# A two-model f32 kernel: norm statistics as four columns, latents read raw by ScalarE, convolution work dealt anew

## What is computed

```python
for l in range(2):
    p = rmsnorm(x, g_mix[l]) @ w_in[l]            # 384 | 256 | 32 | 2 x 512 columns
    c_q, c_kv = rmsnorm(p[:, :384], g_q[l]), rmsnorm(p[:, 384:640], g_kv[l])
    q = c_q @ w_uq[l]; k_nope, v = split(c_kv @ w_ukv[l])
    k_rope = rope(p[:, 640:672]);  a, gt = split(p[:, 672:])
    y_attn = softmax((q . [k_nope, k_rope]) / sqrt(96)) @ v       # 8 heads
    u = dwconv31(a * sigmoid(gt)) + b;  u = silu(layernorm(u))
    x = x + concat(y_attn, u) @ w_o[l]
    z = dwconv3(rmsnorm(x, g_ffn[l]) @ w_up[l]); x = x + (silu(zg) * zv) @ w_down[l]
x = rmsnorm(x, g_final)
```

## Time and profile before

| | us |
|---|---|
| median of 3 runs | 3025.79 |
| lowest and highest | 3019.03, 3028.0 |
| the profiled execution | 3028.47 |
| its span | 3026.7 |
| TensorE matmul busy in the span | 2827.2 (93%) |
| VectorE busy | 1775.7 (59%) |
| GpSimd busy | 1764.7 (58%) |
| ScalarE busy | 777.0 (26%) |

### The profile page before, as it was taken

How to read it: one execution, slowest core, us unless ns; L and a number is a source line. 1 busy time by engine, 2 the same in 40 slices (tenths; PEclk the granted TensorE clock), 3 DMA queues, 4 the chain that set the end, 5 groups by cost and what they waited for, 6 DMA issues and landing times.

```text
span 3026.7 us, 35770 instructions
## 1 busy us (share of the span) xinstructions
PE 2827.2 (93%) x12832; PEld 2291.1 (76%) x12832; DVE 1775.7 (59%) x1941; ACT 777.0 (26%) x1256; POOL 1764.7 (58%) x1000
## 2 busy tenths in 40 slices
PE   6898899999787999989999989999999998899998
PEld 5676788887676888877776778888777777788876
DVE  8884566428855666256656557054666665842644
ACT  2332222102423222023555312011222221310202
POOL 5983566667944766654443447666553343566663
PEclk9998999999998999999999989999999998899999
DMA  3111222232011322322111113222221111232221
GB/s 134 56 43 49 77 97 97 99 104 91 28 36 55 110 95 95 106 79 73 63 63 56 63 65 108 93 95 97 77 90 62 56 56 50 76 99 96 97 98 49
DMA packets 66367, 237.36 MB, mean 78 GB/s; under 512 B 7152, under 2 KB 7408, under 8 KB 66224
## 3 DMA queue, kind: packets, MB, share of 16 engines
q1 hardware_dynamic: 65392, 234.00, 23.2%
q10 hardware_dynamic: 832, 1.51, 0.2%
HBM read 233.38 MB, written 2.10 MB: 78 GB/s over the span
## 4 chain that ended last, share of the span: by engine, by line
PE 77%; DVE 12%; DVEq 5%; issue 3%; ACT 2%; DMA 0%; ACTq 0%; SPq 0%
PE ps L457 23%; PE ps L463 22%; PE ps L460 22%; PE ps L1013 2%; PE ps L579 1%; DVE ps L1594 1%; DVE qw L2224 1%; PE ps L802 1%; DVEq L2226 1%; PE ps L1049 1%; PE ps L805 1%; DVE rstd L1567 1%; DVE ssum L1498 1%; DVE ssum L2072 0%; DVE x_lo L1486 0%
## 5 line engine op out<-in xcount | busy, mean ns | idle before, releaser
L398 POOL TENSOR_SCALAR w_hi<-w_raw 128x1024 fp32r<-128x1024 f32 x437 | 481.2, 1101 | 1193.3 <-PE ps L457 1182.5
L400 POOL TENSOR_TENSOR w_lo<-w_raw,w_hi 128x1024 fp32r<-128x1024 f32 x437 | 1108.8, 2537 | 36.4
L457 PE MATMUL ps<-x_hi,w_hi 128*128 128x512 f32 x2024 | 817.9, 404 | 74.1 <-DVE x_lo L2110 16.3
L463 PE MATMUL ps<-x_hi,w_lo 128*128 128x512 f32 x2024 | 797.8, 394 | 0.0
L460 PE MATMUL ps<-x_lo,w_hi 128*128 128x512 f32 x2024 | 797.8, 394 | 0.0
L457 PEld LDWEIGHTS ps<-x_hi,w_hi 128*128 128x128 f32 x2024 | 386.0, 191 | 177.0 <-issue 33.8
L460 PEld LDWEIGHTS ps<-x_lo,w_hi 128*128 128x128 f32 x2024 | 386.7, 191 | 83.5 <-issue 5.5
L463 PEld LDWEIGHTS ps<-x_hi,w_lo 128*128 128x128 f32 x2024 | 385.9, 191 | 82.9
L457 PE MATMUL ps<-a_hi,w_hi 128*128 128x512 f32 x512 | 201.8, 394 | 0.0
L463 PE MATMUL ps<-a_hi,w_lo 128*128 128x512 f32 x512 | 201.0, 393 | 0.0
L460 PE MATMUL ps<-a_lo,w_hi 128*128 128x512 f32 x512 | 199.2, 389 | 0.0
(11 more groups left out here) (377 smaller groups left out, 4566.6 us busy)
## 6 DMA issues: line engine op xcount, KB each, us to landing
w_raw<-wts SPq DMA_DIRECT2D x437, 512.0 KB, 3.3
xres<-xT SPq DMA_DIRECT2D x2, 1024.0 KB, 8.8
outT<-xres SPq DMA_DIRECT2D x1, 2048.0 KB, 7.1
pf<-pT ACTq DMA_DIRECT2D x2, 512.0 KB, 3.5
prm<-prm SPq DMA_DIRECT2D x1, 452.0 KB, 3.9
lev<-levels ACTq DMA_DIRECT2D x1, 384.0 KB, 3.1
wtmp<-pos SPq DMA_DIRECT2D x1, 128.0 KB, 3.1
ident<-identity SPq DMA_DIRECT2D x1, 64.0 KB, 10.6
```

Of the source, the lines that this page charges most:

```text
L398: nc.gpsimd.tensor_scalar(w_hi[:, s, :], w_raw[:, s, :], 1.0, 0.0, ALU.mult, ALU.add).then_inc(w_rounded[s], 1)
L400: nc.gpsimd.tensor_tensor(w_lo[:, s, :], w_raw[:, s, :], w_hi[:, s, :].bitcast(F32), ALU.subtract).then_inc(w_split[s], 1)
L457: mm = nc.tensor.matmul(out, whi, xhi, start=first, stop=False)
L463: return nc.tensor.matmul(out, wlo, xhi, start=False, stop=last)
```

## The change

Statistics of the first model. The sums are made as four columns: TensorE multiplies the 128x128 pieces of the sum tile by one column of ones (row_stat); root and reciprocal are taken on 128x4 tiles (rowm); TensorE spreads the four factor columns over a bank with the identity (row_factor), and the users read the factor from that bank. For statistic 0 ScalarE copies it to rstd. The spread of statistic 0 stands in the middle of input tile 1, that of 1 behind tile 7, that of 2 behind tile 10, that of 3 behind output block n = 2, that of 4 right behind its sum. The mixer's sum tile is kept in root, since statistics 1 and 2 add a multiple of it.

Latents. The kv and q tiles are taken raw from PSUM by ScalarE, multiplied with their gain (taken), and squared from PSUM too. The mixer's factor drops out of their norm but for the eps, which the added multiple of the sum tile stands for (ecol, ebias). VectorE multiplies them by their factor only.

Convolution. GpSimd has channel tile 2 in place of 1, and its taps are behind blocks 15, 17, 18 and 19. VectorE has 0, 1 and 3; 45 of its 96 steps a layer stand ahead of the first query, where 39 did. The third key tile goes to bank 5 in place of 0.

```diff
@@ -83,10 +83,10 @@
 VW = VDIM + 1
-K_BANK = [2, 3, 0, 1]
-POOL_CH = 1
-CONV_BY_DVE = [0, 2, 3]
-POOL_TAPS = {10: 1, 11: 1, 12: 1, 13: 1, 15: 2, 17: 10, 18: 8, 19: 7}
+K_BANK = [2, 3, 5, 1]
+POOL_CH = 2
+CONV_BY_DVE = [0, 1, 3]
+POOL_TAPS = {15: 3, 17: 12, 18: 9, 19: 7}
@@ -474,8 +476,27 @@
+            def row_stat(out, l, k, extra=None):
+                pe.wait_ge(sum_ready, l * 6 + (k + 1))
+                for tt in range(TT):
+                    c = slice(tt * P, (tt + 1) * P)
+                    mm = nc.tensor.matmul(out[:, tt:tt + 1], (root if k <= 0 else ssum)[:, c], ones[:, 0:1], start=True,
+                                          stop=extra is None)
+                    if extra is not None:
+                        mm = nc.tensor.matmul(out[:, tt:tt + 1], root[:, c], ecol[:, extra, :], start=False, stop=True)
+                mm.then_inc(stat_ready, 1)
+            def row_factor(out, n):
+                pe.wait_ge(root_used, n + 2)
+                for tt in range(TT):
+                    mm = nc.tensor.matmul(out[:, tt * P:(tt + 1) * P], rowm[:, 1, tt:tt + 1].to_broadcast([P, P]), ident[:, :],
+                                          start=True, stop=True)
+                mm.then_inc(factor_ready, 1)
             BU = [0, 0, 0, 0]
-            for n in ([t % 4 for t in range(W_IN)] + K_BANK + [0] * (HEADS + HEADS // 2)
+            for n in ([t % 4 for t in range(W_IN)] + [b for b in K_BANK if b < 4] + [0] * (HEADS + HEADS // 2)
                       + [b for b in W_O_BANK if b < 4] + [m % 4 for m in range(KD + 2 * FT)]):
@@ -490,23 +511,30 @@
                             pe.wait_ge(x_split, l * 2 * KD + (kt + 1))
+                        if t == 1 and kt == 5:
+                            row_factor(ps[4], l * 5)
                         mm = three(ps[b][:, :], w_hi[:, s, kt * P:(kt + 1) * P], w_lo[:, s, kt * P:(kt + 1) * P],
...
                     if t == 0:
-                        stat(ps[4][:, :], l, 0)
+                        row_stat(ps[4], l, 0)
                     if t == 6:
-                        pe.wait_ge(root_ready, l * 5 + 1)
-                        stat(ps[4][:, :], l, 1)
+                        pe.wait_ge(rstd_ready, l + 1)
+                        row_stat(ps[4], l, 1, 0)
+                    if t == 7:
+                        row_factor(ps[4], l * 5 + 1)
+                    if t == T_KR:
+                        pe.wait_ge(kvn_ready, l * KKV + KKV)
+                        row_stat(ps[4], l, 2, 1)
                     if t == T_KR + 1:
-                        pe.wait_ge(root_ready, l * 5 + 2)
-                        stat(ps[4][:, :], l, 2)
+                        row_factor(ps[4], l * 5 + 2)
...
                 for i, b in enumerate(K_BANK):
-                    bank(b, l * BU[b] + 1)
+                    if b < 4:
+                        bank(b, l * BU[b] + 1)
                     for kt, s in ((0, s0), (1, s1)):
@@ -649,10 +677,12 @@
                     if n == 1:
-                        stat(ps[7][:, :], l, 4)
-                pe.wait_ge(root_ready, l * 5 + 4)
-                stat(ps[4][:, :], l, 5)
+                        row_stat(ps[7], l, 4)
+                    if n == 2:
+                        row_factor(ps[7], l * 5 + 3)
+                row_stat(ps[4], l, 5)
+                row_factor(ps[4], l * 5 + 4)
                 first_up = []
@@ -1096,32 +1125,44 @@
-                def sqrt(bank, k, n, widen=1):
+                def sqrt(bank, k, n, bias, widen=1):
...
                     act.wait_ge(root_used, lr + (k + 1))
-                    nc.scalar.activation(root[:, :], bank, ACT.Sqrt, bias=(epsc if widen == 1 else epsq)[:, :],
-                                         scale=widen / n).then_inc(root_ready, 1)
-                sqrt(ps[4][:, :], 0, D)
+                    nc.scalar.activation(rowm[:, 0, :], bank[:, 0:TT], ACT.Sqrt, bias=bias, scale=widen / n).then_inc(root_ready, 1)
+                def taken(t, dst, gain, i, n):
+                    act.wait_ge(acc_ready, l * A_ALL + (A_IN + t + 1))
+                    nc.scalar.activation(dst, ps[t % 4][:, :], ACT.Identity, scale=gain)
+                    square(i, n, ps[t % 4][:, :])
+                    act.drain().then_inc(acc_free[t % 4], 1)
+                sqrt(ps[4], 0, D, epsc[:, :])
+                act.wait_ge(factor_ready, lr + 1)
+                nc.scalar.activation(rstd[:, :], ps[4][:, :], ACT.Copy).then_inc(rstd_ready, 1)
                 def sigmoid(c):
...
                 sigmoid(1)
-                for i in range(KKV):
-                    act.wait_ge(kvf_ready, l * KKV + (i + 1))
-                    square(i, lq + i, kvf[:, i, :])
-                sqrt(ps[4][:, :], 1, KV_LORA)
+                def kv_in(i):
+                    taken(T_KV + i, kvf[:, i, :], prm[:, pc + (L_GKV + i), :], i, lq + i)
+                def q_in(i):
+                    taken(T_Q + i, cqf[:, i, :], prm[:, pc + (L_GQ + i), :], i, lq + (KKV + i))
+                kv_in(0)
+                kv_in(1)
+                q_in(0)
+                sqrt(ps[4], 1, KV_LORA, ebias[:, 0, :])
+                q_in(1)
                 act.wait_ge(kvn_ready, l * KKV + KKV)
...
                     nc.scalar.activation(kv_hi[:, i, :], kvf[:, i, :], ACT.Copy).then_inc(kv_round, 1)
-                for i in range(KQ):
-                    act.wait_ge(cqf_ready, l * KQ + (i + 1))
-                    square(i, lq + (KKV + i), cqf[:, i, :])
-                sqrt(ps[4][:, :], 2, Q_LORA, QK)
+                q_in(2)
+                sqrt(ps[4], 2, Q_LORA, ebias[:, 1, :], QK)
                 act.wait_ge(kr_ready, l + 1)
@@ -1562,10 +1606,8 @@
-                    dve.drain()
                     dve.wait_ge(root_ready, l * 5 + (k + 1))
-                    V.reciprocal(rstd[:, :], root[:, :]).then_inc(root_used, 1)
-                    dve.drain()
+                    V.reciprocal(rowm[:, 1, :], rowm[:, 0, :]).then_inc(root_used, 1)
@@ -1618,6 +1660,7 @@
                 inverse(0)
+                dve.wait_ge(rstd_ready, l + 1)
                 V.tensor_tensor(wtmp[64:128, :], rope_cs[64:128, :], rstd[64:128, :], ALU.mult)
@@ -1625,49 +1668,30 @@
                 gate_a(1, 2)
-                conv(7)
+                conv(6)
                 gate_g(1, 3)
...
                 gated(1)
+                conv(3)
+                add_square(0, False, lq, l * 6 + 1)
+                conv(6)
+                add_square(1, True, lq + 1, l * 6 + 1)
                 conv(4)
-                def kv_in(i):
-                    evacuate(kvf[:, i, :], T_KV + i).then_inc(kvf_ready, 1)
-                    dve.drain().then_inc(acc_free[(T_KV + i) % 4], 1)
-                kv_in(0)
+                inverse(1)
                 conv(5)
-                kv_in(1)
+                add_square(0, False, lq + KKV, l * 6 + 2)
+                dve.wait_ge(factor_ready, l * 5 + 2)
                 for i in range(KKV):
-                    conv(1)
-                    add_square(i, i == KKV - 1, lq + i, l * 6 + 1)
-                def q_in(i):
-                    evacuate(cqf[:, i, :], T_Q + i).then_inc(cqf_ready, 1)
-                    dve.drain().then_inc(acc_free[(T_Q + i) % 4], 1)
-                conv(4)
-                q_in(0)
-                dve.wait_ge(root_ready, l * 5 + 2)
-                V.reciprocal(qf[:, :], root[:, :]).then_inc(root_used, 1)
-                dve.drain()
-                for i in range(KKV):
-                    V.scalar_tensor_tensor(kvf[:, i, :], kvf[:, i, :], prm[:, pc + (L_GKV + i), :], qf[:, :], ALU.mult,
-                                           ALU.mult).then_inc(kvn_ready, 1)
-                q_in(1)
+                    V.tensor_tensor(kvf[:, i, :], kvf[:, i, :], ps[4][:, :], ALU.mult).then_inc(kvn_ready, 1)
+                conv(1)
                 for i in range(KKV):
...
                     V.tensor_tensor(kv_lo[:, i, :], kvf[:, i, :], kv_hi[:, i, :].bitcast(F32), ALU.subtract).then_inc(kv_split, 1)
-                dve.drain()
+                add_square(1, False, lq + KKV + 1, l * 6 + 2)
                 V.memset(mrow[:, :, :].bitcast(F32), 0.0).then_inc(mrow_zero, 1)
-                for i in range(2):
-                    add_square(i, False, lq + (KKV + i), l * 6 + 2)
-                conv(1)
-                q_in(2)
-                conv(1)
-                add_square(2, True, lq + (KKV + 2), l * 6 + 2)
-                conv(3)
+                conv(2)
+                add_square(2, True, lq + KKV + 2, l * 6 + 2)
+                conv(4)
                 acc(A_IN + T_KR)
@@ -1676,13 +1700,11 @@
                 V.tensor_tensor(qf[64:128, :], qf[64:128, :], a_sb[64:128, :], ALU.add).then_inc(kr_ready, 1)
+                inverse(2)
                 conv(1)
-                dve.wait_ge(root_ready, l * 5 + 3)
-                V.reciprocal(wtmp[:, :], root[:, :]).then_inc(root_used, 1)
-                dve.drain()
+                dve.wait_ge(factor_ready, l * 5 + 3)
                 for i in range(KQ):
```

(60 more changed lines are left out.)

6 lines of the change are left out of this document (3 added, 3 removed).

## The result

The change makes the kernel slower: 3031.55 us (median of 15, 3027.53 to 3033.54) against 3023.51 us before (15 runs), ratio 1.0023, 95% interval 1.0016 to 1.0031. The forecast was 3002 us. The profiled execution has a span of 3029.2 us.

What follows compares the result with a forecast made beforehand. VectorE arriving late at the hand-over from input projection to attention, and bare chains such as that ahead of the FFN, bound it. Terms: -17 - 2 + 1.6 - 4.4 - 2.0 = -23.8 us, giving 3002 us, range 2990 to 3015.

Steps and rivals of the forecast that it cites:

- part 3: Convolution norm: factor's spread queued behind 24 output projection matmuls, so products start later; +0.8 us a layer, bounds +1.2 and -3.
- The step on GpSimd's cover: Attention: block 19 split at 194, query 6 needing it at about 200, so 6 us of cover left.
- part 2: Attention: VectorE enters with six taps fewer, shortening the wait before a query tile; 1 us a layer gained, 2 in all.
- Rival D: Attention: query tiles wait for GpSimd beyond 3.2 us a tap; 3044 us at 4.2 us a tap; chance 0.03.
- Part 1: Input projection to first query: less VectorE work, so query 0 is read earlier; 8.5 us a layer, 17 for both.
- rival B: Input projection: late sums or spreads stop TensorE's queue and take half the gain; 3012 us; chance 0.15.
- Part 4: Norm ahead of the FFN and final norm: shorter chain; 2.2 us a layer, 4.4 for two, and 2.0 for the final norm.
- rival C: Shorter waits at the norms leave TensorE's clock at 2.4 GHz, some 4 us more per place; 2994 us; chance 0.10.
- Rival E: Input projection to first query bound by something else ending as before, for instance ScalarE's rotary copies; 3020 us; chance 0.07.
- The charge for a PSUM source: Norm products reading PSUM: 120 cycles against 58 for SBUF, 0.065 us on some 25 products, 1.6 us a layer.

Runs made afterwards that it cites:

- taps: pad32 with GpSimd's taps behind blocks 15, 17, 18, 19 dealt 3, 8, 8, 12 in place of 3, 12, 9, 7; 3002.50 us, ratio 0.9921.
- pad32: The changed kernel with 32 unused bytes put back in front of the big SBUF region; 3014.91 us, ratio 0.9963.
- spread3: pad32 with the spread of the convolution norm's factor behind output block 1 in place of 2; 3004.54 us, ratio 0.9931.
- kbank: The kernel of taps with the third key tile back in bank 0; 3010.01 us, ratio 0.9955.

## Why the prediction was wrong, step by step

Wrong in sign: -23.8 us were forecast and +8 measured. Two things account for it; a third, part 3, was mis-sized.

**The step on GpSimd's cover failed (part 2).** The clock of GpSimd was counted well: block 19's split was forecast at 194 and ended at 195.3, the taps "near 214" ended at 214.0. The date that it was held against was wrong. The prediction took the wait at 209.52 for that of query 6. It is that of query 7, which uses the same block; query 6 ran at 196.50 before. Moved 9 us forward it needs block 19 near 187.5, so by the prediction's own clock there were over 6 us missing in place of "6 us of cover", and query 4 was late as well. The waits are 1.58 and 4.46 us, and the clock fell to the lower of its two levels behind each (granted 0.50 from 167 to 169 us and from 195.4 to 199). Rival D named this mechanism, with a wrong point of decision: 3.2 us a tap, where 2.9 was already too slow. Priced by taps against pad32: 12.4 us.

**The change was read as having no part in the layout.** The prediction goes through every instruction and not through the allocations. The 32 bytes cost 16 to 18 us, more than the late weights. By the traces of the change and of pad32, 9.2 us of that lie in the second model and 4.5 in the two down projections. Nothing in the prediction covers that; no rival names it.

**Part 3 was mis-sized in the change.** Its mechanism, the factor's spread that stands behind 24 matmuls, and its sign were right. But from the sum to the first matmul on the convolution's output it took 13.75 us (252.61 to 266.36) where it took 11.21 before (256.32 to 267.53): 2.5 us more in each layer, where +0.8 was forecast and +1.2 the bound. The clock fell to 0.50 between 255.0 and 258.3 us, behind a wait of 1.30 us at the sum. In pad32, behind a wait of 1.40, it stays at 1.00 and the stretch takes 12.13 us, +0.9, close to the forecast. In taps it stays up in layer 0 and falls in layer 1, behind waits of the same length. What decides between the two is open.

With the late weights and the addresses taken away the kernel runs at 0.9921 of the kernel before, which is 24 us less: the sum of the prediction, 23.8. That the sum fits so well is partly luck, since its terms were off in both directions:

- Part 1 was right. Query 0 was to be read "near 124.3" and is read at 125.35, 8.15 us earlier than before, where 8.5 was taken. Query weights at "121.5": the matmul starts at 122.25, released by GpSimd as forecast. No wait in the key projection, clock at full. The lateness of the sums and spreads (rival B) was not seen: TensorE has no wait at those of the kv and q norms. The key bank is worth more than the prediction gave it: 3.3 us in layer 0's trace and 10 us in the ratios of kbank and taps.
- Part 2 gave attention 1 us a layer. In taps the output projection of layer 0 starts 9.1 us ahead of the kernel before (230.97 for 240.08), 2.0 more than query 0 is read ahead (126.43 for 133.50).
- Part 3's bound of -3 was out of reach with the spread where the change has it. With the spread one block earlier (spread3) 4.0 us a layer came back.
- Part 4: the spread ran at the halved clock, 2.09 us in the chain, so that the gain is 6.79 - 5.20 = 1.6 a layer, not 2.2; at the final norm it is 1.8 (7.78 us from sum to first matmul before, 6.02 after), where 2.0 was forecast. The page cited for rival C, TensorE: Matmul & The Clock Gate (Why this matters for your kernels) in the Trainium skill, speaks of a long idle stretch. In this chain the lower level came behind waits of only 2.30 and 1.92 us, and at query 4 behind one of 1.58.
- Rival E fell with the first query, which came earlier.

The charge for a PSUM source in the Trainium skill's VectorE: DVE Perf Modes (The TRN2 errata), which the prediction set against the change, is still not borne out: four products with the factor in PSUM take 2.72 us, where they took 2.74 from SBUF.

## What to carry to other kernels

When work ahead of a consumer shrinks, every queue that feeds the consumer later has a new due date: list each use of each split block with its own start in the trace of before, and move all of them forward, not only the first. And when a change adds or drops a tile, compare the addresses of everything behind it; the spacing of matmuls at full clock, to a nanosecond, is the row that shows the difference, and a few bytes of padding are tried in one run. A small result that is ready early helps only if its next instruction is not queued behind a block of matmuls, as the norm's factor was here.

## What the runs showed of the hardware that was not expected

The spacing of 512-column f32r matmuls at the full granted clock went with the distance in SBUF between the stationary and the moving tile: 226.7 to 227.1 ns at the three distances that are multiples of 256 bytes (two of them of 512), 228.9 to 233.3 ns at the others. Moving both by 32 bytes changed nothing, moving one did. At 320 modulo 512 two values were seen, so something beside the distance has a part there. In this kernel 32 bytes are 0.4 to 0.6% of the time. Why this is so is open, and so is what the distances do that no run had (160, 192 and 224 modulo 256).
